# A 128-byte constant tile moved from ahead of the token tiles to behind them in on-chip memory

## The chip, the cores and the metric

The kernel runs on one core of one Trainium2 chip. The metric is the device time of one execution in microseconds; three runs of the kernel before were taken, and one more execution was profiled.

## The reference, cut to what matters

The reference takes 256 tokens of width 1024 (all fp32) through two transformer blocks.

```
def reference(x, ...):
    x = first_block(x, ...)    # norm; h @ w_in; mLSTM and sparse attention; two gated branches;
                               # @ w_out; norm; SwiGLU with a hidden width of 2816; final norm
    return second_block(x, mem, ...)  # norm; h @ w_in_2; linear attention, indexed attention,
                               # memory attention; three gated branches; @ w_out_2; norm;
                               # mixture of 16 experts
```

Nearly all arithmetic is products of 256 tokens with weight matrices that are read once from HBM. Each root-mean-square norm needs a power of minus one half, and that is the only use of the tile that the change moves.

## The kernel before, in words

**Slabs.** Each large weight matrix is streamed in slabs of 1024 rows by 256 columns, 1 MB each (`[P, KT, SW]`: 128 partitions by 8 pieces of the contraction by 256 columns, 8 KB in each partition). SyncE loads a slab into `ring`, ScalarE copies it rounded to fp32r into `w_hi` (`high`, line 578), VectorE writes the rest into `w_lo` (`low`, line 591), which lies on the memory of `ring`. The tokens are split in the same way into `xT_hi` and `xT_lo` (transposed: 128 partitions of features, 8 pieces, 256 tokens). A product is then three TensorE matmuls (`product`, line 616): hi by hi, hi by lo, lo by hi. All of them carry line 620 in the profile.

**Which operand stands and which moves.** In a matmul the stationary operand of 128 by 128 is loaded into the array by its own instruction (LDWEIGHTS, the row PEld), while the matmul ahead of it runs, and the moving operand of 256 or 512 columns streams past it. In the profile's names the moving one comes first: `bank<-xT_hi,w_hi` moves tokens past weights, `bank<-w_hi,xT_hi` moves weights past tokens. There are three ways to use a slab:

- `slab_rows` (line 627): weights stationary, tokens moving, 256 columns, 48 matmuls a slab. This is used for the query, key, merge, indexer and gate slabs, for gate and up of the first block's SwiGLU (`units_pe`, line 955), and with other moving tiles for the branch products: `ysT`, `o_m`, `o_g`, `o_d`.
- `slab_tokens` (line 642): tokens (or `mixT`, `merged`) stationary, weights moving, 256 columns, 48 matmuls.
- `slab_wide` (line 654): tokens or memory stationary, weights moving, 512 columns, 24 matmuls a slab.

The SwiGLU runs 11 units: a gate slab and an up slab by `slab_rows`, then a down slab whose moving weights pass the hidden tile `h` in 512 columns. The mixture of experts at the end does the same with gathered tokens `xgs`, `xgo` and `turned_h`, never with `xT`.

**Order.** It is written out by hand, in program order for each engine, with semaphores between them; there is no planner. TensorE's program starts at line 2546. SyncE issues the slab loads in the order of `STREAM`, each when the slab that held its slot has been used.

**Addresses.** Tiles that live all through the kernel are allocated one behind the other by `sb` (lines 153 to 177), and `place` (line 180) lays the other tiles over the memory behind `w_hi` at an offset. From the shapes, in bytes per partition: `ident` to `ones` take 4096 bytes, `minus_half` 128, `rows` and `cols` 1024 each, `x`, `xn`, `xT_hi` and `xT_lo` 8192 each, `ss` 64, then `w_lo` 32768 and `w_hi` 24576. So `xT_hi` begins at 22656 and `xT_lo` at 30848 (both 128 modulo 256), and `w_lo` at 39104 and `w_hi` at 71872 (both 192 modulo 256). All later tiles count from 96448, which is 192 modulo 256 too. Several of them carry hand-set offsets:

```
mixT_hi = place(64, "mixT_hi", [P, KT, T], F32R)
APART = [0, 0, 0, 64, 64, 64, 64, 64, 256, 256, 320]
EIGHT = [8 * KB + 8448 + 4608 + 8 * KB * i + APART[i] for i in range(11)]
```

With these, `o_m`, `o_g`, `o_d`, `merged`, `mixT_hi` and `ysT_lo` begin at 0 modulo 256, `mixT_lo` and `ysT_hi` at 128, and `h`, `memT`, `xgs`, `xgo` and `turned_h` at 192, as the weights do.

**The tile that moves.** `minus_half` is `[P, 32]`, 128 bytes. GpSimd fills it once (line 1160) and reads it in the roots of the norms (`norm_root`, line 746; `head_root`, line 938; line 1206). `x` and `xn` hold the tokens and their normed copy, which TensorE transposes into `xT`.

Of the kernel before, what the change touches and what calls it, by code (L numbers as in the profile page):

```python
# [14 lines left out]
P = 128  # L15
# [115 lines left out]
def program(nc, dram, out, plan):  # L131
# [3 lines left out]
    def sb(name, shape, dtype=F32, into=None):  # L135
        return (into or ctx).enter_context(nc.sbuf_tensor(name, shape, dtype))
# [23 lines left out]
    ones_r = sb("ones_r", [P, P], F32R)  # L160
    causal = sb("causal", [P, T])
    ones = sb("ones", [P, P])
    minus_half = sb("minus_half", [P, 32])
    rows = sb("rows", [P, 2, P])
    cols = sb("cols", [P, 2, P])
    x = sb("x", [P, TT, D])
# [3 lines left out]
        xT_raw = sb("xT_raw", [P, KT, T], into=into)  # L170
    xT_lo = sb("xT_lo", [P, KT, T], F32R)
    ss = sb("ss", [P, 8 * TT])
    raw_ctx = ExitStack()
    ring = sb("ring", [P, RAW, KT, SW], into=raw_ctx)
    raw_ctx.close()
# [2977 lines left out]
```

How the kernel before makes its waits and increments, by code:

```python
    def evicted(eng, s):  # L548
        for w in all_out(s):
            eng.wait_ge(*w)
# [1 line left out]
    def slab_out(eng, name, j=0):  # L552
        eng.wait_ge(slab_used, SLAB[name] + j + 1)
# [23 lines left out]
    def high(act, end):  # L578
        for s in range(split["hi"], end):
            act.wait_ge(*loaded(s))
            if HI <= s < MOE + HI:
                act.wait_ge(slab_used, s - HI + 1)
            elif MOE + HI <= s < MOE + MORE_HI:
                act.wait_ge(*moe_pe.done("gather", KT - 1))
            elif s >= HI:
                act.wait_ge(slab_used, s - MORE_HI + 1)
            for k in halves(s):
                act.activation(HIGHS[HI_SLOT[s]][:, k, :], RAWS[SLOT[s]][:, k, :], ACT.Copy).then_inc(w_hi_ready, 1)
        split["hi"] = max(split["hi"], end)
# [1 line left out]
    def low(vec, end):  # L591
        for s in range(split["lo"], end):
            for n, k in enumerate(halves(s)):
                vec.wait_ge(w_hi_ready, parts_of(s, n))
                vec.tensor_tensor(LOWS[SLOT[s]][:, k, :], RAWS[SLOT[s]][:, k, :], HIGHS[HI_SLOT[s]][:, k, :].bitcast(F32),
                                  ALU.subtract).then_inc(w_lo_ready, 1)
        split["lo"] = max(split["lo"], end)
# [8 lines left out]
    def slab_in(pe, s):  # L607
        pe.wait_ge(w_lo_ready, parts_of(s, 0))
        if s in BANKED and BANKED[s] >= 2:
            pe.wait_ge(bank_read[BANKED[s] % 2], 2 * (BANKED[s] // 2))
# [1 line left out]
    def second_half(pe, s):  # L613
        pe.wait_ge(w_lo_ready, parts_of(s, 1))
# [432 lines left out]
    @block.sync  # L1047
# [96 lines left out]
            if name == "kv":  # L1144
                sp.wait_ge(loads["rev"], 16)
```

## Time and profile before

| | us |
|---|---|
| median of 3 runs | 1015.41 |
| lowest and highest run | 1014.60 and 1018.62 |
| the profiled execution, its own time | 1016.27 |
| its span, first to last instruction | 1015.0 |
| TensorE matmuls busy in it | 995.4 (98%) |
| weight loads busy in it | 897.7 (88%) |
| VectorE, ScalarE busy in it | 680.8, 585.2 |
| mean granted TensorE clock | 0.997 of full speed |

The profile is one execution. Busy matmul time counts a matmul from its start to its modelled end, and matmuls overlap, so how fast TensorE goes is read from the distance between the starts of two matmuls (called the pace below), not from busy time or from the duration of one. 0.86 us lie between the profiled execution's own time and the median.

### The profile page before, as it was taken

The page shows a single profiled execution, that of the slowest core. Times are in us where ns is not written, and L with a number is a line of the kernel's source. Part 1 is how long each engine was busy: PE and PEld are TensorE (multiplying, and loading weights), DVE is VectorE, ACT ScalarE, POOL GpSimd, SP SyncE. Part 2 cuts the span into 40 slices and gives each one's busy share as a digit, 9 for nine tenths or more (in the row PEclk, how much of TensorE's full clock was granted, in tenths as well). Part 3 has the DMA queues.
Part 4 walks back from the last instruction along what each step waited for, and adds up shares of the span by engine and source line. Part 5 has one row for each costly group of instructions (what it writes and reads, how often), then busy time and mean ns, then how long its engine had stood idle before and what let it go on. Part 6 is the DMA issues. An engine that isn't in the chain of part 4 may idle for free.

```text
span 1015.0 us, 16341 instructions
## 1 busy us (share of the span) xinstructions
PE 995.4 (98%) x6730; PEld 897.7 (88%) x6730; DVE 680.8 (67%) x1019; ACT 585.2 (58%) x855; POOL 44.0 (4%) x57
## 2 busy tenths in 40 slices
PE   6999999999999999999999999999999989999998
PEld 6998988999999999889898878998999978888886
DVE  5865767677555545586575665656556768998887
ACT  5564576756343433374585545675444548877774
POOL 4101000000000000010010001100000000000001
PEclk9999999999999999999999999999999989999999
DMA  9994543357655556564453333553565928999995
GB/s 263 262 304 130 151 156 125 126 169 209 198 182 192 190 184 198 178 217 144 147 167 125 124 125 125 166 172 125 167 205 174 314 96 275 367 371 371 369 367 198
DMA packets 168248, 206.31 MB, mean 203 GB/s; under 512 B 11431, under 2 KB 143118, under 8 KB 168174
## 3 DMA queue, kind: packets, MB, share of 16 engines
q1 hardware_dynamic: 159598, 196.01, 59.3%
q0 software_dynamic: 2224, 6.07, 2.0%
q10 hardware_dynamic: 6352, 3.19, 1.2%
q8 instruction: 53, 0.87, 0.4%
q14 instruction: 21, 0.17, 0.1%
HBM read 201.56 MB, written 4.73 MB: 203 GB/s over the span
## 4 chain that ended last, share of the span: by engine, by line
PE 89%; DVE 3%; DMA 3%; ACT 2%; issue 1%; SPq 1%; POOL 0%; ACTq 0%; DVEq 0%; POOLq 0%
PE bank L620 76%; PE bank L757 1%; PE bank L813 1%; DVE w_lo L596 1%; DMA ring<-in_w_in 1%; PE bank L3038 1%; DMA ring<-in_w_up 1%; PE bank L803 1%; ACT w_hi L588 1%; PE bank L2631 1%; PE bank L2715 1%; DMA ring<-in_w_out 1%; PE bank L2770 1%; PE bank L2732 1%; DMA x<-in_x 1%
## 5 line engine op out<-in xcount | busy, mean ns | idle before, releaser
L596 DVE TENSOR_TENSOR w_lo<-ring,w_hi 128x1024 fp32r<-128x1024 f32 (+1 forms) x302 | 423.0, 1436 | 176.5 <-ACT w_hi L588 176.0
L588 ACT ACTIVATE w_hi<-ring 128x1024 fp32r<-128x1024 f32 (+1 forms) x302 | 357.6, 1225 | 184.4 <-PE bank L620 141.8
L620 PE MATMUL bank<-xT_hi,w_hi 128*128 128x256 f32 x896 | 253.4, 283 | 0.0
L620 PE MATMUL bank<-xT_lo,w_hi 128*128 128x256 f32 x896 | 250.8, 280 | 0.0
L620 PE MATMUL bank<-xT_hi,w_lo 128*128 128x256 f32 x896 | 250.8, 280 | 0.0
L620 PEld LDWEIGHTS bank<-xT_hi,w_hi 128*128 128x128 f32 x896 | 169.1, 189 | 2.5 <-issue 1.6
L620 PEld LDWEIGHTS bank<-xT_hi,w_lo 128*128 128x128 f32 x896 | 170.8, 191 | 0.0
L620 PEld LDWEIGHTS bank<-xT_lo,w_hi 128*128 128x128 f32 x896 | 169.0, 189 | 0.8 <-issue 0.2
L620 PE MATMUL bank<-w_hi,xT_hi 128*128 128x512 f32 (+1 forms) x208 | 77.7, 373 | 0.3 <-ACT cmp_in L1309 0.3
L620 PE MATMUL bank<-w_hi,xT_lo 128*128 128x512 f32 (+1 forms) x208 | 76.2, 366 | 0.0
L620 PE MATMUL bank<-w_lo,xT_hi 128*128 128x512 f32 (+1 forms) x208 | 75.8, 364 | 0.0
L620 PE MATMUL bank<-w_hi,xgs_hi 128*128 128x512 f32 x128 | 51.5, 402 | 0.0
L620 PE MATMUL bank<-w_hi,xgs_lo 128*128 128x512 f32 x128 | 50.1, 391 | 0.0
L620 PE MATMUL bank<-w_lo,xgs_hi 128*128 128x512 f32 x128 | 49.9, 390 | 0.0
L620 PEld LDWEIGHTS bank<-w_hi,xT_hi 128*128 128x128 f32 x208 | 39.1, 188 | 8.0 <-issue 1.9
L620 PEld LDWEIGHTS bank<-w_hi,xT_lo 128*128 128x128 f32 x208 | 39.1, 188 | 6.7
L620 PEld LDWEIGHTS bank<-w_lo,xT_hi 128*128 128x128 f32 x208 | 39.1, 188 | 6.2
L620 PE MATMUL bank<-w_hi,h_hi 128*128 128x512 f32 x88 | 34.2, 389 | 0.0
L620 PE MATMUL bank<-w_lo,h_hi 128*128 128x512 f32 x88 | 34.2, 389 | 0.0
L620 PE MATMUL bank<-w_hi,h_lo 128*128 128x512 f32 x88 | 34.2, 389 | 0.0
L620 PE MATMUL bank<-w_hi,turned_hi 128*128 128x512 f32 x80 | 31.2, 390 | 0.0
L620 PE MATMUL bank<-w_hi,turned_lo 128*128 128x512 f32 x80 | 31.1, 389 | 0.0
(549 smaller groups left out, 1797.3 us busy)
## 6 DMA issues: line engine op xcount, KB each, us to landing
ring<-in_w_in SPq DMA_DIRECT2D x54, 1024.0 KB, 5.2
ring<-in_w_down SPq DMA_DIRECT2D x31, 1024.0 KB, 7.1
ring<-in_w_gate SPq DMA_DIRECT2D x40, 512.0 KB, 7.3
ring<-in_w_up SPq DMA_DIRECT2D x40, 512.0 KB, 8.8
ring<-in_w_gate SPq DMA_DIRECT2D x11, 1024.0 KB, 5.3
ring<-in_w_up SPq DMA_DIRECT2D x11, 1024.0 KB, 5.4
ring<-in_w_out SPq DMA_DIRECT2D x8, 1024.0 KB, 5.1
ring<-in_w_mem_kv SPq DMA_DIRECT2D x8, 1024.0 KB, 5.1
```

The lines of the kernel that those rows point to most:

```text
L588: act.activation(HIGHS[HI_SLOT[s]][:, k, :], RAWS[SLOT[s]][:, k, :], ACT.Copy).then_inc(w_hi_ready, 1)
L596: vec.tensor_tensor(LOWS[SLOT[s]][:, k, :], RAWS[SLOT[s]][:, k, :], HIGHS[HI_SLOT[s]][:, k, :].bitcast(F32), ALU.subtract).then_inc(w_lo_r ...
L620: ins = pe.matmul(dst, a, b, start=(start and j + m == 0), stop=(stop and j == len(pairs) - 1 and m == 2), **kw)
L757: ins = pe.transpose(bank[4 + k // 2][:, at:at + P], src[:, t, k * P:(k + 1) * P], ident[:, :])
L803: ins = pe.matmul(dst, a, b, start=(i == 0), stop=(i == len(parts) - 1))
L813: ins = pe.matmul(dst, a, b, start=(i == 0), stop=(i == len(parts) - 1))
L2631: ins = mm_(bank[3][0:NG * NCMP, j * P:(j + 1) * P], blk[:, j, n, :, :].rearrange("p g c -> p (g c)"), w_cmp1[:, j, n, :], start=(n == 0), ...
L2715: ins = mm_(bank[4 + odd][:, i * K:(i + 1) * K], nqT[odd * ND:(odd + 1) * ND, h // 2, tt * P:(tt + 1) * P], kT[odd * ND:(odd + 1) * ND, br ...
L2732: ins = mm_(dst[odd], v_sw[:, kt, b, g * ND:(g + 1) * ND], aT[:, b, kt, 2 * odd:2 * odd + 2, :], start=False, stop=(b == 1 and kt == tt))
L2770: ins = pe.transpose(nsa_turned(u, kt)[:, i * P:(i + 1) * P], lg_nsa(u)[:, i, kt * P:(kt + 1) * P], ident[:, :])
L3038: ins = mm_(bank[GATHER_BANK[k]][:, :], v[:, t, k * P:(k + 1) * P], onehot[:, t, 0:NGRP, :].rearrange("p g s -> p (g s)"), start=(t == 0 a ...
```

## The change

`minus_half` is no longer allocated between `ones` and `rows`, but between `ss` and the weight ring. Nothing else differs: no instruction, wait, loop or shape.

```diff
@@ -160,7 +160,6 @@
     ones_r = sb("ones_r", [P, P], F32R)
     causal = sb("causal", [P, T])
     ones = sb("ones", [P, P])
-    minus_half = sb("minus_half", [P, 32])
     rows = sb("rows", [P, 2, P])
     cols = sb("cols", [P, 2, P])
     x = sb("x", [P, TT, D])
@@ -170,6 +169,7 @@
         xT_raw = sb("xT_raw", [P, KT, T], into=into)
     xT_lo = sb("xT_lo", [P, KT, T], F32R)
     ss = sb("ss", [P, 8 * TT])
+    minus_half = sb("minus_half", [P, 32])
     raw_ctx = ExitStack()
     ring = sb("ring", [P, RAW, KT, SW], into=raw_ctx)
     raw_ctx.close()
```

Seven tiles (`rows`, `cols`, `x`, `xn`, `xT_hi`, `xT_lo`, `ss`) begin 128 bytes lower, at 22528 and 30720 for the two token tiles (0 modulo 256). The weight tiles and everything behind them stay where they are.

## Rows read from the trace of the kernel before

**Rows 1.** The page: busy time by engine, then the chain that ended last.
```profile
PE 995.4 (98%) x6730; PEld 897.7 (88%) x6730; DVE 680.8 (67%) x1019; ACT 585.2 (58%) x855; POOL 44.0 (4%) x57
...
PE 89%; DVE 3%; DMA 3%; ACT 2%; issue 1%; SPq 1%; POOL 0%; ACTq 0%; DVEq 0%; POOLq 0%
```
**Rows 2.** The chain in order of time: start, us, what.
```profile
234.63 216.92 PE bank L620 x1464
...
712.73 94.05 PE bank L620 x816
```
**Rows 3.** Line 620 on TensorE, 239.9 to 428.9 (SwiGLU): ns min/median/max, first and last start.
```profile
L620 PE MATMUL bank<-xT_lo,w_hi x352: 281/281/281, 240.1 to 413.0; 128*128 128x256 f32 x176
```
**Rows 4.** TensorE's timeline, ends of four SwiGLU slabs (192 matmuls), then the down slab.
```profile
239.95 0.28 PE L620 MATMUL bank<-xT_hi,w_hi 128*128 128x256 f32 x1
...
262.44 0.28 PE L620 MATMUL bank<-xT_hi,w_lo 128*128 128x256 f32 x1
262.56 0.39 PE L620 MATMUL bank<-w_hi,h_hi 128*128 128x512 f32 x1
...
267.77 0.39 PE L620 MATMUL bank<-w_hi,h_lo 128*128 128x512 f32 x1
```
**Rows 5.** Line 620, 712.9 to 790.2 (gate and branch slabs by turns), columns as in rows 3.
```profile
L620 PE MATMUL bank<-xT_lo,w_hi x112: 276/276/279, 712.7 to 784.4; 128*128 128x256 f32 x112
...
L620 PE MATMUL bank<-o_d_lo,w_hi x64: 280/280/280, 751.4 to 790.0; 128*128 128x256 f32 x64
```
**Rows 6.** TensorE's timeline: ends of one branch slab and of one gate slab in there.
```profile
718.02 0.28 PE L620 MATMUL bank<-o_g_hi,w_hi 128*128 128x256 f32 x1
...
723.56 0.28 PE L620 MATMUL bank<-o_g_hi,w_lo 128*128 128x256 f32 x1
...
724.02 0.28 PE L620 MATMUL bank<-xT_hi,w_hi 128*128 128x256 f32 x1
...
729.01 0.28 PE L620 MATMUL bank<-xT_hi,w_lo 128*128 128x256 f32 x1
```
**Rows 7.** Line 620 in four other stretches: 55 to 66, 654 to 666, 673 to 678, 597 to 602.
```profile
L620 PE MATMUL bank<-xT_lo,w_hi x32: 276/276/281, 55.1 to 65.7; 128*128 128x256 f32 x32
...
L620 PE MATMUL bank<-xT_lo,w_hi x32: 281/281/281, 654.5 to 665.5; 128*128 128x256 f32 x32
...
L620 PE MATMUL bank<-o_m_lo,w_hi x16: 276/276/276, 673.1 to 678.2; 128*128 128x256 f32 x16
...
L620 PE MATMUL bank<-w_lo,xT_hi x16: 277/279/279, 596.7 to 602.0; 128*128 128x256 f32 x16
```
**Rows 8.** Groups by form: weights moving past tokens and past `merged`, mean ns last.
```profile
L620 PE MATMUL bank<-w_hi,xT_hi 128*128 128x512 f32 x160 | 64.0, 400 | 0.0
...
L620 PE MATMUL bank<-w_lo,merged_hi 128*128 128x256 f32 x64 | 17.7, 277 | 0.0
```
**Rows 9.** TensorE's timeline in a wide slab: weights moving past tokens, 42 matmuls apart.
```profile
535.03 0.39 PE L620 MATMUL bank<-w_lo,xT_hi 128*128 128x512 f32 x1
...
544.64 0.39 PE L620 MATMUL bank<-w_lo,xT_hi 128*128 128x512 f32 x1
```
**Rows 10.** Matmuls of tokens past weights in the whole trace, columns as in rows 3.
```profile
L620 PE MATMUL bank<-xT_lo,w_hi x896: 276/281/415, 12.9 to 784.4; 128*128 128x256 f32 x180
```
**Rows 11.** The view of the moved tile: its largest reader, columns as in rows 3.
```profile
L748 POOL TENSOR_TENSOR ss<-ss,minus_half x6: 695/705/1601, 7.7 to 818.5; 128x2 f32<-128x2 f32 x6
```
**Rows 12.** Windows: us, PE, PEld, DVE, ACT, POOL busy (count), clock, DMA share, GB/s.
```profile
234.60:451.50 216.90, 216.90 (x1467) 200.91 (x1465) 126.81 (x149) 97.01 (x123) 1.39 (x2) 1.00 0.61 194
712.70:806.80 94.10, 94.10 (x819) 94.10 (x818) 56.87 (x73) 43.60 (x57) 0.00 (x0) 1.00 0.66 212
850.00:971.00 121.00, 121.00 (x547) 99.17 (x545) 108.55 (x88) 94.53 (x86) 1.62 (x3) 1.00 1.07 368
```
**Rows 13.** TensorE's timeline at the start of a gate slab.
```profile
647.30 0.29 PE L620 MATMUL bank<-xT_lo,w_hi 128*128 128x256 f32 x1
...
647.55 0.28 PE L620 MATMUL bank<-xT_hi,w_hi 128*128 128x256 f32 x1
```

## The prediction

> **What bounds the kernel now.** I read the page first: TensorE's matmuls are busy for 98% of the span, and the chain of work that ended last is TensorE for 89% [rows 1]. The chain in order of time then shows stretches with nothing but line 620 in them, above all 216.92 us from 234.63 and 94.05 us from 712.73 [rows 2]. The windows over these say that no other engine is near its limit there: VectorE 127 of 217 us, DMA 0.61, and full clock [rows 12]. So whatever changes the pace of TensorE's matmuls there changes the end by as much. In the mixture of experts, DMA share is 1.07 [rows 12], but its matmuls read neither token tile except in a short gather, and its loads wait for slots that TensorE frees, so time won or lost ahead of it passes through.
>
> The change has no instruction in it, so the only thing to look for is whether the time of an operation depends on its addresses. The view of line 620 is to be read for that. One form of matmul, tokens past weights in 256 columns, has two durations in steady running, 276 and 281 ns, with a median of 281 over 896 [rows 10]. All 352 of the SwiGLU are at 281 exactly [rows 3], all of the gate slabs from 712.9 at 276 [rows 5]. The timeline turns this into paces. In the SwiGLU, from 239.95 to 262.44 there are 191 steps, 117.7 ns each [rows 4]. In the gate slab, 724.02 to 729.01 is 44 steps, 113.4 ns each [rows 6]. So the same form on the same tiles runs at a **fast pace** of 113.4 or a **slow pace** of 117.7 ns, 4.3 ns or 0.21 us for a slab of 48. Going by the starts of all slabs one by one, 20.2 of the 56 token slabs run fast: 8.2 of 16 ahead of the SwiGLU, none of its 22, 5 of the 11 between 458 and 712, all 7 from 712.9. A slab keeps its pace from a few matmuls after its start to its end: the two from 55 on are fast, the two from 654 on slow [rows 7]. Something set at the start of a run thus chooses between two paces, and a slab at 113.4 leaves nothing more to win.
>
> **What distance the tiles have.** I write r for moving minus stationary address modulo 256, in bytes. Tokens past weights have r = -64 now (128 against 192) and +64 after (0 against 192). Weights past tokens have +64 now and -64 after. Branch tiles past weights already have +64, weights past `merged` already have -64; both also agree with the tokens after the change modulo 1024. `h`, `memT` and the gathered tokens have 0 and keep it. So the trace of before already holds the two new distances, on other tiles, and the forecast can be made from those.
>
> **The change part by part.**
>
> *The tile itself.* GpSimd reads `minus_half` in thirteen small operations, six of them of about 0.7 us [rows 11]. They are the same after. I cost its new place at nothing either way; 128 bytes more or less in an address add no work to an operation of two columns. If even 0.1 us came on each, at most one microsecond would show, and part of that beside TensorE work.
>
> *Tokens past weights, slabs that are fast now.* Of slabs with r = +64, the branch slabs are one fast, `o_m` at 673 [rows 7], and eleven slow (`o_g`, `o_d` at 279 to 280 ns [rows 5], and from 718.02 to 723.56 47 steps of 117.9 ns [rows 6]). Of three slabs of weights past tokens in 256 columns, also +64, one is fast and two are slow, as the one from 597 to 602 [rows 7]. That makes 2 fast of 15. The bounds are that all 20.2 fast token slabs stay fast (0) and that all turn slow (20.2 x 0.21 = 4.2 us). I take the share of the branch slabs: 2.7 stay, 17.5 turn, **+3.7 us**.
>
> *Tokens past weights, slow now.* These are 35.8 slabs, 22 of them in the SwiGLU, where each pair follows the down slab with r = 0. No row shows a step from r = 0 to r = +64. Bounds: none turns fast (0), or all do (35.8 x 0.21 = -7.5 us; the SwiGLU alone -4.6). By the nearest rows, the 2 of 15, I take 4.7 slabs, **-1.0 us**.
>
> *Weights past tokens, 512 columns.* There are 480 such matmuls, three groups like the one of 160 [rows 8]. Their pace is 9.61 us over 42 steps, 228.8 ns [rows 9], against 5.21 over 23, 226.5 ns, with r = 0 [rows 4]. At most 2.3 ns each can go, 1.1 us. Nothing shows 512 columns at r = -64, so the other bound is that they get worse by as much. `merged` in 256 columns with r = -64 is at 277 ns on average [rows 8], fast for the three slabs that follow each other, so I lean to a gain and take half, **-0.5 us**.
>
> *Weights past tokens, 256 columns.* Three slabs, two slow now; at the rate of `merged` (three fast of four) this gives **-0.2 us**, between -0.4 and +0.2.
>
> *Everything else that moves.* `x` and `xn` are read in transposes and by VectorE and ScalarE, which have slack [rows 12]; I take 0. The waits stay the same, and ahead of each stall stands the same producer.
>
> Sum: +3.7 - 1.0 - 0.5 - 0.2 = **+2.0 us**. Against the profiled execution's own 1016.27 (span 1015.0, 1.3 around it) that is 1018.3. The median of the runs is 0.86 lower, so 1015.41 + 2.0 gives **1017.4**.
>
> **A page that speaks against any effect.** In this trace the same form has the paces 113.4 and 117.7 on the same tiles, and 228.8 against 226.5 on different ones [rows 4, 6, 9]. The Trainium skill, page "TensorE: Matmul & The Clock Gate", section "Step-by-step: what each phase is for", says that TensorE has two independent read ports, one for the moving operand and one for the weight load, so that the load takes no bandwidth from the running matmul. By that, the distance of two tiles could not matter and the sum would be 0. No row here shows the ports themselves; that the 512-column pace differs by tile in all fifteen runs of weights past tokens speaks against it.
>
> **The rivals.**
>
> *The fast pace wins in the SwiGLU.* The step from `h` or `memT` (r = 0) to tokens now always ends in the slow pace, 11 of 11, and the step from fast tokens (r = -64) to a branch tile (r = +64) too, 7 of 7. So what counts is phase and distance together, and a phase that clashes at -64 need not at +64. With tokens and branches at one distance, the back and forth from 718 on goes as well. If only the SwiGLU turns fast and the fast ones elsewhere turn slow: -4.6 + 3.7 - 1.1 - 0.2 (weights past tokens) = -2.2, 1013.2. If all 256-column slabs with tokens or branches run fast: -7.5 - 2.3 (eleven branch slabs) - 0.4 - 1.1 = -11.3, 1004.1. The middle is 1008.7. For it: 36 of 56 token slabs have something to win and only 20 to lose. Against it: 13 of 15 slabs with +64 are slow.
>
> *Nothing happens.* Distance has no say, and the pace is set by the waits alone, which stay: 1015.4. For it: the same tiles show both paces. Against it: the 7-by-7 alternation, which follows the tile at every boundary.
>
> *Slower, by a third pace.* The place is the SwiGLU. A gate slab shows 647.30 to 647.55 for two steps, 125 ns [rows 13], as it starts; it is gone after some matmuls, because it falls back. If r = +64 after r = 0 held that pace, the 22 slabs would lose 22 x 48 x 7.3 ns = 7.7 us: with the rest 1025. It decides the sign from 3 ns a matmul on (3.2 us, which brings the sum to 5.1). Against it: no slab holds this pace, at any distance.
>
> **How the numbers follow.** Forecast 0.43, fast SwiGLU 0.31, nothing 0.13, third pace 0.13. About 5 us, 0.5%, is what a measurement can tell from no change. The forecast's bounds are 1012 to 1020, nearly all of it within 0.5%. Of the 0.31, some 0.25 lies below 1010.3, since it needs more than the SwiGLU alone. Slower by over 0.5% are 0.12 of the third pace and 0.03 of the forecast. That makes faster 0.26, same 0.59, slower 0.15. The range from 1005 to 1021 leaves out the last of the all-fast case and most of the third pace, under 0.2 together; the forecast's own range is 1012 to 1020.
>
> **What would show each step.** In the profile after: the duration of tokens past weights over the SwiGLU (281 now; a value near 280 says slow at the new distance, 276 fast, above 285 the third pace), and its pace from the first and last start of a slab. From 712.9 on, whether gate slabs join the branch slabs at 279 to 280 or draw them to 276. The wide slabs: 226.5 or 228.8. The median of all 896. And the stretch of 216.92 us in the chain: 221 or more refutes the forecast on one side, under 214 on the other. Should all paces stay while the time moves, the cause is elsewhere, in the first load or in `xn`, and the whole working is wrong.

## The result, and the profile after

Ten runs of each kernel: before 1018.19 us in the median (1014.35 to 1019.23), after 1022.97 (1020.29 to 1023.99). The ratio is 1.006, with a 95% interval from 1.0048 to 1.0072: by it the change makes the kernel slower by 6.1 us (4.9 to 7.3). (The two medians lie 4.8 us apart and the two means 5.4, so 5 to 6 us is what these runs support.) The change was taken again at the end, as one of the experiments, and gave 1.0061. The prediction had no measurable change as likeliest, +2.0 us, with an upper end of its range at 1021. It was wrong: the measured 1022.97 lies 2 us above that end. (The median of before was 2.8 us higher in these ten runs than in the three that the prediction had. The two groups of times that the clock makes, below, are the likely reason, but no clock is on record for these ten; against those three, the ratio gives 1021.5, which is outside too.)

The instructions on each engine are the same and stand in the same order. The profiled execution has an own time of 1023.99 and a span of 1022.7, against 1015.0 before. The page of after, against [rows 1]: the engines' busy times and the chain by engine.

```profile
PE 1003.6 (98%) x6730; PEld 902.6 (88%) x6730; DVE 681.2 (67%) x1019; ACT 585.5 (57%) x855; POOL 44.2 (4%) x57
...
PE 94%; DMA 2%; DVE 2%; ACT 1%; issue 1%; SPq 1%; POOL 0%; DVEq 0%; ACTq 0%; POOLq 0%
```

VectorE, ScalarE and GpSimd are busy for the same time within 0.4 us, TensorE for 8.2 us more, with the same 6730 matmuls. So nearly all of the extra time lies in matmuls and not in waits.

The SwiGLU in the chain in order of time (start, us, what), against [rows 2]:

```profile
236.34 217.29 PE bank L620 x1464
```

It is 0.4 us longer only. The window over it (columns as in rows 12) says the same as [rows 12]: VectorE, ScalarE and DMA are far from their limits, at full clock.

```profile
236.00:455.00 219.00, 219.00 (x1483) 202.63 (x1481) 128.30 (x151) 98.67 (x125) 1.71 (x3) 1.00 0.61 193
```

Line 620 on TensorE: first the whole trace, then 241.5 to 431.6 (SwiGLU), then 716.7 to 795.9 (gate and branch slabs by turns). Columns as in rows 3; the answers to [rows 10], [rows 3] and [rows 5].

```profile
L620 PE MATMUL bank<-xT_lo,w_hi x896: 276/279/415, 12.9 to 790.1; 128*128 128x256 f32 x180
...
L620 PE MATMUL bank<-xT_lo,w_hi x352: 279/279/281, 241.7 to 415.1; 128*128 128x256 f32 x176
L620 PE MATMUL bank<-w_hi,h_hi x88: 389/389/402, 264.2 to 431.0; 128*128 128x512 f32 x88
...
L620 PE MATMUL bank<-xT_lo,w_hi x112: 278/280/280, 717.0 to 790.1; 128*128 128x256 f32 x112
L620 PE MATMUL bank<-o_d_lo,w_hi x64: 280/280/280, 756.5 to 795.7; 128*128 128x256 f32 x64
```

The SwiGLU stays slow (281 became 279, but that is the duration of one matmul, not the distance of starts: that comes below). The gate slabs from 717 on went from 276 to 280, all seven. Among the token slabs the fast pace is gone but for parts of two, at 160 and 167 us.

TensorE's timeline of after, as in [rows 4] and [rows 9]: the same matmuls by their number in the program, in the SwiGLU, at the start of the down slab behind it, and in a wide slab.

```profile
241.63 0.28 PE L620 MATMUL bank<-xT_hi,w_hi 128*128 128x256 f32 x1
...
264.13 0.28 PE L620 MATMUL bank<-xT_hi,w_lo 128*128 128x256 f32 x1
264.25 0.40 PE L620 MATMUL bank<-w_hi,h_hi 128*128 128x512 f32 x1
264.49 0.39 PE L620 MATMUL bank<-w_lo,h_hi 128*128 128x512 f32 x1
264.71 0.39 PE L620 MATMUL bank<-w_hi,h_lo 128*128 128x512 f32 x1
264.94 0.40 PE L620 MATMUL bank<-w_hi,h_hi 128*128 128x512 f32 x1
...
537.87 0.39 PE L620 MATMUL bank<-w_lo,xT_hi 128*128 128x512 f32 x1
...
547.67 0.39 PE L620 MATMUL bank<-w_lo,xT_hi 128*128 128x512 f32 x1
```

In the SwiGLU 22.50 us for 191 steps is 117.8 ns, exactly the slow pace of before. In the wide slab 9.80 us for 42 steps is 233.3 ns, where it was 228.8: **4.5 ns more on a matmul, and this was forecast to fall.** The down slab starts with steps of 240 and 220 ns, and its first eight are 231 ns in the mean, where its own pace is 227.

Summed over the trace, by the mean step of each form (steps inside slabs, stalls left out), after minus before: tokens past weights 116.3 to 117.7 ns, 2688 matmuls, +3.8 us; weights past tokens in 512 columns 229.3 to 233.3, 480 matmuls, +1.9; `h` 226.7 to 228.1, 264 matmuls, +0.4; one `o_m` slab +0.2; weights past tokens in 256 columns -0.2; `merged` -0.2. The sum is +5.9. The gate slabs' last matmul of tokens starts at 790.1 where it was 784.4 [rows 5], 5.7 us later. So the slabs account for the whole difference up to there.

The other 2 us of the span difference of 7.7 come after the last norm, and they go with the clock. Windows of after there (columns as in rows 12):

```profile
824.00:834.30 10.30, 6.64 (x19) 5.42 (x19) 7.86 (x21) 3.98 (x5) 1.10 (x1) 0.50 0.21 69
...
846.00:849.00 3.00, 3.00 (x19) 2.72 (x19) 2.09 (x7) 2.98 (x3) 0.39 (x1) 0.83 0.74 186
849.00:852.00 3.00, 3.00 (x9) 2.33 (x9) 1.75 (x1) 0.37 (x1) 1.12 (x2) 0.60 0.48 165
```

The same place of the profiled execution before:

```profile
820.80:827.60 6.80, 5.25 (x15) 4.33 (x16) 5.19 (x13) 1.22 (x4) 0.00 (x0) 0.50 0.01 2
...
828.00:866.00 38.00, 38.00 (x196) 31.95 (x195) 33.59 (x60) 29.80 (x35) 1.51 (x2) 1.00 0.64 217
```

TensorE waits around the norm and the router there (busy for 29.7 of 34 us from 800.0 in after, 28.7 of 33 from 795.0 in before), the granted clock falls to 0.50 (1.2 GHz), and it comes back to 1.00 (2.4 GHz) after 6.8 us in this execution of before and after 10.2 us, with a second dip of 3.4 us from about 848, in the one of after. The mean granted clock of a run, 0.997 for this execution of before and 0.993 for this one of after, varies from run to run in **both** kernels. Over all runs whose clock is on record, before has 35 runs at 0.997 with a mean of 1015.7 us, 33 at 0.993 with 1018.3, and 20 in between; after has 3 at 0.997 with 1020.6, 6 at 0.993 with 1023.7, and 8 in between. At equal clock the change costs 4.9 us in the one case and 5.3 in the other. Against the runs of before that were taken beside it, the repetition (e15 below) gives 5.5 us at 0.997 (2 runs against 9) and 5.8 at 0.993 (2 against 7). That is near the 5.9 of the slabs. Only 3 of the 17 runs of after had 0.997, and 35 of 88 of before; whether the change makes these rarer isn't shown by so few.

### The profile page after: what moved, and what is told of

The parts are those of the page before. It is cut to its first block, busy times and chain, and to the rows that moved or that the text cites. A ratio compares the mean times of both kernels' runs of the same rounds, so it can differ in the third digit from the quotient of the medians.

```text
span 1022.7 us, 16341 instructions
## 1 busy us (share of the span) xinstructions
PE 1003.6 (98%) x6730; PEld 902.6 (88%) x6730; DVE 681.2 (67%) x1019; ACT 585.5 (57%) x855; POOL 44.2 (4%) x57
## 4 chain that ended last, share of the span: by engine, by line
PE 94%; DMA 2%; DVE 2%; ACT 1%; issue 1%; SPq 1%; POOL 0%; DVEq 0%; ACTq 0%; POOLq 0%
PE bank L620 80%; PE bank L757 1%; PE bank L813 1%; PE bank L803 1%; PE bank L3038 1%; DMA ring<-in_w_up 1%; PE bank L2631 1%; PE bank L2715 1%; DMA ring<-in_w_out 1%; PE bank L2770 1%; PE bank L2732 1%; DMA x<-in_x 1%; SPq L1128 0%; PE bank L2940 0%; PE bank L2945 0%
## 5 line engine op out<-in xcount | busy, mean ns | idle before, releaser
L620 PEld LDWEIGHTS bank<-xT_hi,w_lo 128*128 128x128 f32 x896 | 168.7, 188 | 0.0
```

Source lines behind the costliest of these rows:

```text
L620: ins = pe.matmul(dst, a, b, start=(start and j + m == 0), stop=(stop and j == len(pairs) - 1 and m == 2), **kw)
```

## The experiments

In the theory after the result, the distance r of the moving from the stationary tile, modulo 256 bytes, sets which paces a matmul can have, and the tile's move costs through the tokens' r alone. Its rivals are the absolute place of the tiles; the place of `x`, `xn` or of `minus_half` itself; the entry into a slab rather than its distance. The experiments were run in four groups. Ratios are against runs of the kernel before in the same group; its median was 1017.47, 1016.37, 1017.17 and 1015.89 us in the four. Of each kernel one execution was profiled, and all paces come from that one. "The slabs' sum" is the sum by mean steps, as above. (The addresses given ahead of the prediction count from the first tile; only distances enter below.)

### First group: which tile, and is it distance?

**e1_all_up**: everything from `rows` on lies 128 bytes higher, all distances kept. The small tile `ik_sq`, which then found no room at its place, lies on other free memory in this and the other kernels that take up more.

```diff
+    sb("gap1", [P, 32])
-    ik_sq = place(EXTRA + 4 * KB, "ik_sq", [P, TT, IDIM])
+    ik_sq = place(EXTRA, "ik_sq", [P, TT, IDIM])
```

> Everything from rows on lies 128 bytes higher than before, so the tokens have the absolute address class they have after the change, but their distance to the weights is that of before (-64). Theory 1 (the distance of tokens to weights modulo 256 sets the pace): same as before, ratio 0.998 to 1.002, about 20 of 56 token slabs fast, wide slabs at 228.9 ns. Theory 2 (the address of the tokens itself counts): ratio 1.006, all token slabs slow, wide slabs at 233.3 ns. (ik_sq, one small tile, lies on the memory of score to make room.)

Measured: 0.9975 (0.9965 to 0.9985), not slower. Its tokens keep their two paces, against [rows 10] and, below, [rows 8]:

```profile
L621 PE MATMUL bank<-xT_lo,w_hi x896: 276/281/287, 12.7 to 783.1; 128*128 128x256 f32 x180
...
L621 PE MATMUL bank<-w_hi,xT_hi 128*128 128x512 f32 x160 | 64.1, 401 | 0.0
```

20.1 of 56 token slabs are fast (20.2 before), and the wide slabs take 229.6 ns (229.3). The absolute place modulo 256 isn't the cause. The 2.4 us that it gained in the median are not in the slabs (their sum is -0.2 us) and partly in the clock: at 0.997 the difference is 1.4 us (1014.9 against 1016.3). What the rest is stays open (e14 below has the same shift).

**e2_x_xn**: `minus_half` between `xn` and `xT_hi`, so `rows`, `cols`, `x` and `xn` move, and the token tiles don't.

```diff
-    minus_half = sb("minus_half", [P, 32])
     rows = sb("rows", [P, 2, P])
...
     xn = sb("xn", [P, TT, D])
+    minus_half = sb("minus_half", [P, 32])
```

> minus_half stands between xn and xT_hi: only rows, cols, x and xn lie 128 bytes lower, the token tiles and weights stay. Theory 1: ratio 0.998 to 1.002, token slabs as before. Theory 3 (the new place of x and xn, whose transposes precede many stretches, sets the pace that follows): ratio 1.004 or more, and the slabs that follow transposes slow.

Measured: 1.0011 (0.9995 to 1.0028). The wide slabs take 229.2 ns; 13.5 instead of 20.2 token slabs are fast, +0.9 us by the slabs' sum. Neither the tile's own place nor that of `x` and `xn` makes the change's cost. But the choice between the two paces is touched by something other than distance: the seven gate slabs from 711 us on, fast in every other profile with the tokens at -64, are all slow in this one. One profiled execution can't tell whether the place of `x` and `xn` does that or the execution.

**e3_hi_only**: `minus_half` between `xT_hi` and `xT_lo`: only `xT_hi` goes to r = +64.

```diff
+    minus_half = sb("minus_half", [P, 32])
     xT_lo = sb("xT_lo", [P, KT, T], F32R)
```

> minus_half stands between xT_hi and xT_lo: x, xn and xT_hi lie 128 lower, xT_lo stays, so two of three matmuls have the new distance and one the old. Theory 1: if each matmul pays for its own distance, two thirds of the loss, ratio 1.004, wide slabs at about 231.8 ns (two thirds of the way from 228.9 to 233.3). If the mixture itself decides, as in ysT (hi -64, lo +64 for moving tiles), all moving token slabs at 117.8 and a ratio near 1.005.

Measured: 1.0045 (1.0031 to 1.0059), 4.6 us, with 4.9 by the slabs' sum. No token slab is at 113.4 ns: 24 run at 117.0, among them all 22 of the SwiGLU, and 32 at 117.8. The wide slabs take 231.7 ns. Two thirds of the matmuls read `xT_hi`, and three quarters of the change's cost by the ratios (4.6 of 6.1 us) are there.

**e4_r0**: the tokens at the distance zero from the weights.

```diff
+    sb("gap1", [P, 16])
...
     ss = sb("ss", [P, 8 * TT])
+    sb("gap2", [P, 48])
```

> Tokens and weights at one place modulo 256 (r = 0), as h and memT are. Theory 1 by the rows of before: wide slabs fall from 228.9 to 226.7 ns (-1.1 us); the token slabs of 256 columns are open: all fast would be -7.5 us more (ratio 0.992), all slow +4.2 (ratio 1.003). Theory 2: at least as slow as after or unrelated.

Measured: 1.0067 (1.0041 to 1.0093). The timeline of this kernel, the same matmuls as in [rows 4] and [rows 9]:

```profile
242.78 0.28 PE L622 MATMUL bank<-xT_hi,w_hi 128*128 128x256 f32 x1
...
265.69 0.28 PE L622 MATMUL bank<-xT_hi,w_lo 128*128 128x256 f32 x1
...
541.22 0.39 PE L622 MATMUL bank<-w_lo,xT_hi 128*128 128x512 f32 x1
...
550.76 0.39 PE L622 MATMUL bank<-w_lo,xT_hi 128*128 128x512 f32 x1
```

119.9 ns in 256 columns, worse than either pace of before; 227.1 ns in 512 columns, better than before. This is the clearest result for distance: one shift moves the two forms in opposite directions, and the wide slabs take the pace that `h` has at r = 0 (226.7).

### Second group: modulo what, and are other tiles alike?

**e5_r128**: r = 128 for the tokens. **e6_plus_256**: the weights and all behind them 256 bytes up.

```diff
-    minus_half = sb("minus_half", [P, 32])     # e5
+    minus_half = sb("minus_half", [P, 16])
...
+    sb("gap2", [P, 16])
...
     ss = sb("ss", [P, 8 * TT])                 # e6
+    sb("gap2", [P, 64])
```

> minus_half 64 bytes long and 64 bytes behind ss: tokens 128 from the weights (r = 128 = -128), everything behind ss in place. Theory 1 (distance modulo 256, a table of paces by r: tokens moving 116.3 ns on average at -64, 117.8 at +64, 119.9 at 0; weights moving in 512 columns 226.7 at 0, 228.9 at +64, 233.3 at -64): a fourth entry, different from the others on both. If only the fraction of 64 mattered (theory 4), it would equal r = 0: 119.9 and 227.

> Weights and all behind them 256 bytes higher, tokens in place: distance -64 - 256. Theory 1 with 256 as the modulus: as before, about 20 token slabs fast, wide slabs 228.9 ns, ratio 0.998 to 1.002. If the modulus is 512 or more, other paces, wide slabs away from 228.9.

Measured: e5 1.0083 (1.0055 to 1.0112), 119.3 ns and 232.6 ns. e6 0.9995 (0.9977 to 1.0013), 116.3 ns and 229.3 ns, the paces of before to the tenth of a nanosecond. So 256 bytes are a period of the effect (64 is not one, by e4, nor 128, by the change itself).

**e7_h_plus64**: the tokens as before, the hidden tile `h` moved from 0 to +64.

```diff
-    h_hi, h_lo = (place((4 + 2 * i) * KB, "h_" + n, [P, 2, T], F32R) for i, n in enumerate(("hi", "lo")))
+    h_hi, h_lo = (place(EXTRA + 128 + 2 * KB * i, "h_" + n, [P, 2, T], F32R) for i, n in enumerate(("hi", "lo")))
```

> Before, with only the SwiGLU's hidden parts h_hi and h_lo in another place, where weights past h have r = +64 instead of 0. Theory 1 with the entry: what runs ahead decides which pace the tokens take. Before, the wide slabs with r = +64 were followed by token slabs twice, and both went fast; slabs with r = 0 were followed by slow ones 11 of 11 times. So the 22 SwiGLU slabs turn fast (-4.6 us) and h pays 264 x 2.3 ns (+0.6): ratio 0.996. If the entry doesn't matter, the SwiGLU stays at 117.8 and the ratio is 1.001.

Measured: 1.0004 (0.999 to 1.0019). Line 620 on TensorE, 262 to 429:

```profile
L620 PE MATMUL bank<-xT_lo,w_hi x289: 280/281/282, 261.7 to 413.1; 128*128 128x256 f32 x145
...
L620 PE MATMUL bank<-w_hi,h_hi x87: 392/392/398, 262.0 to 428.4; 128*128 128x512 f32 x87
```

`h` takes nearly the steady pace of the tokens at that distance, 229.1 ns against 228.8 (229.8 in the mean, 226.7 before). So 512 columns at +64 cost 2.2 to 2.5 ns more than at 0 on both tiles. And the SwiGLU's tokens, which now follow slabs at +64, are still all slow: the tile ahead does not decide it. The query-key slab at 66 us turned slow and the token slab at 108 fast, though `h` is first read at 262: which of the two paces a slab takes can differ without any change of its distance.

**e8_branch_minus64**: the branch tiles moved to the tokens' old distance, r = -64.

```diff
-    APART = [0, 0, 0, 64, 64, 64, 64, 64, 256, 256, 320]
+    APART = [0, 0, 0, 192, 192, 192, 192, 192, 256, 256, 448]
-    merged_lo = place(EIGHT[4], "merged_lo", [P, KT, T], F32R)
+    merged_lo = place(EIGHT[4] - 128, "merged_lo", [P, KT, T], F32R)
-    merged_hi = place(EIGHT[6], "merged_hi", [P, KT, T], F32R)
+    merged_hi = place(EIGHT[6] - 128, "merged_hi", [P, KT, T], F32R)
```

(`w_hi_more` and `xgs` take 192 off where they took 64, so that they stay.)

> Before, with the branch results o_m, o_g, o_d 128 bytes further, so that as moving tiles they have r = -64, the distance that tokens have; merged and the gathered tokens keep theirs. Theory 1: the distance works on any tile, so the eight branch slabs from 705 on turn fast as the gate slabs between them, -1.7 us, ratio 0.998, duration 276 instead of 279 to 280. Rival: the pace belongs to something else in the branch slabs, and they stay at 117.8.

Measured: 1.0000 (0.9984 to 1.0016). All eight slabs of `o_g` and `o_d` went fast, from 117.8 to 113.4 ns (-1.7 us); the one fast `o_m` slab turned slow, and `merged`, whose distance is unchanged, fell from three fast slabs of four to an average of 117.3 (+0.5). So a branch tile can hold the fast pace at -64, but part of the win was lost by the choice between two paces elsewhere. That the distance of the branch tile itself made them fast isn't shown: in e11 of the next group seven of the same eight slabs are fast too, with their distance left at +64.

### Third group: the table by distance

**e9_r_m32, e10_r_m96, e11_r_p32, e12_r_p96**: the tokens at -32, -96, +32 and +96, by paddings ahead of `rows` (gap1) and behind `ss` (gap2), which leave the weights where they were or 256 bytes up, for example e11:

```diff
+    sb("gap1", [P, 24])
...
     ss = sb("ss", [P, 8 * TT])
+    sb("gap2", [P, 40])
```

(e9 has 8 and 56; e10 shortens `minus_half` to `[P, 24]` with 8 behind; e12 puts 8 in the place of `minus_half` and `[P, 16]` of it with 8 more behind `ss`.)

> Tokens 32 bytes below the weights (r = -32 for moving tokens). Theory 1a (between the measured distances the pace lies between theirs): moving tokens on average between 116.3 (-64) and 119.9 (0), about 118.1 ns; wide slabs, r = +32, between 226.7 and 228.9, about 227.8; time about +3 us against before, ratio 1.003. Theory 1b (only whole steps of 64 bytes matter, the lower or the upper neighbour): either the numbers of -64 or those of 0 on both.

> Tokens 96 bytes below the weights (r = -96). Theory 1a: moving tokens between 116.3 (-64) and 119.3 (128), about 117.8 ns; wide slabs between 228.9 and 232.6, about 230.7; ratio 1.004. Theory 1b: the numbers of -64 or those of 128.

> Tokens 32 bytes above the weights (r = +32). Theory 1a: moving tokens between 119.9 (0) and 117.8 (+64), about 118.8 ns; wide slabs, r = -32, between 226.7 and 233.3, about 230; ratio 1.005. Theory 1b: the numbers of 0 or those of +64.

> Tokens 96 bytes above the weights (r = +96). Theory 1a: moving tokens between 117.8 (+64) and 119.3 (128), about 118.5 ns; wide slabs between 233.3 and 232.6, about 233; ratio 1.007. Theory 1b: the numbers of +64 or those of 128.

Measured, with the other runs in one table. "By paces" is the sum over all forms as in the first section, "by ratio" the ratio of the runs times 1015.4, and "equal clock" the difference of mean times against before in the same group, at the mean clock that has the most runs of the kernel (in brackets: runs of the kernel, runs of before; the row of after uses e15 there). r is that of tokens past weights; weights past tokens have minus r. "Steady" are the paces to which the 56 token slabs settle.

```
kernel   r     tokens past w   steady        w past tokens   by paces   by ratio (95%)         equal clock
               256 col, ns     ns            512 col, ns     us         us                     us
before  -64    116.3           113.4, 117.8  229.3
e4        0    119.9           120.0         227.6           + 9.8      + 6.8 ( 4.2 to  9.4)   + 8.3 (3, 9)
e11     +32    116.9           116.7, 117.8  233.2           + 3.2      + 1.0 (-0.3 to  2.2)   + 2.1 (6, 5)
after   +64    117.7           117.8         233.3           + 6.0      + 6.1 ( 4.9 to  7.3)   + 5.5 (2, 9)
e12     +96    120.0           120.0         234.2           +12.6      +11.9 (10.1 to 13.8)   +11.8 (3, 6)
e5      128    119.3           118.7, 119.9  232.6           +10.3      + 8.4 ( 5.6 to 11.4)   + 9.5 (4, 12)
e10     -96    118.3           117.3, 118.7  233.3           + 9.0      + 7.7 ( 5.4 to 10.2)   + 8.7 (2, 6)
e9      -32    118.3           118.3         233.3           + 7.8      + 7.9 ( 5.6 to 10.2)   + 7.9 (3, 6)
```

The fast pace of 113.4 ns is held by about 20 token slabs before and by no whole token slab at any other distance; after has it in parts of two. The sum by paces lies above the ratio's interval for e4 and e11, and within 1.5 us of the difference at equal clock for all.

Line 622 of e11 on TensorE, 715 to 792 (columns as in rows 3), against [rows 5]: the slabs of `o_g` and `o_d`, whose distance is +64 as before, are fast from 721 on, all seven.

```profile
L622 PE MATMUL bank<-o_d_lo,w_hi x63: 276/276/276, 753.9 to 791.8; 128*128 128x256 f32 x63
...
L622 PE MATMUL bank<-o_g_lo,w_hi x48: 276/276/276, 720.7 to 747.9; 128*128 128x256 f32 x48
```

They give e11 1.4 us of its sum back. So +64 allows the fast pace as -64 does, and what a slab takes there depends on more than its own distance; here the gate slabs between them run at 116.7.

The timelines of e11 and of e12, the same stretch of the SwiGLU as in [rows 4]; first e11, 22.29 us for 191 steps, 116.7 ns:

```profile
241.35 0.28 PE L622 MATMUL bank<-xT_hi,w_hi 128*128 128x256 f32 x1
...
263.64 0.28 PE L622 MATMUL bank<-xT_hi,w_lo 128*128 128x256 f32 x1
```

Then e12, in the SwiGLU and in the wide slab of [rows 9]; 120.0 ns, and 9.84 us for 42 steps, 234.3 ns:

```profile
243.36 0.28 PE L622 MATMUL bank<-xT_hi,w_hi 128*128 128x256 f32 x1
...
266.29 0.28 PE L622 MATMUL bank<-xT_hi,w_lo 128*128 128x256 f32 x1
...
542.71 0.39 PE L622 MATMUL bank<-w_lo,xT_hi 128*128 128x512 f32 x1
...
552.55 0.39 PE L622 MATMUL bank<-w_lo,xT_hi 128*128 128x512 f32 x1
```

Both theories of the expectations fail: the paces neither run evenly between their neighbours nor go in steps of 64 bytes: 32 bytes from -64, in either direction, is slow. For 512 columns there are two good distances, 0 and +64 of weights from tokens, and every other one tried costs 232.6 to 234.2. For 256 columns the old distance, -64, has the best mean of the eight, because there token slabs fall into the fast pace of 113.4; +32 has a third stable pace of 116.7 all through the SwiGLU. Of the eight distances tried, the kernel before lies at the one that is good for both forms.

### Fourth group: a version better than both

**e13_branch_merged**: as e8, without the two lines of `merged`, so that weights move past it at +64. **e14_branch_merged_up**: the same with e1's 128 bytes ahead of `rows`. **e15_after_again**: the change once more.

```diff
-    APART = [0, 0, 0, 64, 64, 64, 64, 64, 256, 256, 320]
+    APART = [0, 0, 0, 192, 192, 192, 192, 192, 256, 256, 448]
```

> Before with the branch results at the tokens' distance (-64, as in the run before this kind) and merged at +64 for the weights that move past it. Theory: the eight branch slabs from 705 on stay fast (-1.7 us); merged follows fast slabs, and if +64 suits it as the query-key slabs of weights past tokens at 66, its three slabs in a row are fast again (-0.6): ratio 0.998. Rival: merged goes slow at +64 as most slabs do there, and the ratio stays near 1.000.

> The same with everything from rows on 128 bytes higher, the shift that by itself gave a ratio of 0.9975. If that shift gives something of its own, the two add to 0.996; if its gain was the share of executions with the shorter half-speed stretch of TensorE's clock, the ratio equals that of the kernel without the shift, and the extra shows only in the mean clocks of its runs.

> The changed kernel once more beside before on one chip. Theory 1: in runs of equal mean clock (0.997, or 0.993) it is 5 us slower, which the paces of its slabs give; the rest of the 6 us is the share of runs with the lower clock. Rival: the loss itself is a clock loss, and at equal clock the two kernels are within 2 us.

Measured: e13 0.9987 (0.9972 to 1.0001), 1014.72 against 1015.89 us. e14 0.9991 (0.9976 to 1.0006), so the gain of e1's shift does not come back in the ratio; eight of its 12 runs had the lower clock of 0.993, and against before at that clock it is 2.3 us faster (8 runs against 7). e15 1.0061 (1.0039 to 1.0082), with the paces 117.6, 233.3 and 228.1 ns, where the first profile of after has 117.7, 233.3 and 228.1. One token slab, at 116 us, is at 113.4 here and was at 117.8 there: in the same kernel the choice between the two paces can differ from one execution to the next. Line 620 of e13 from 711 to 790, against [rows 5]:

```profile
L620 PE MATMUL bank<-xT_lo,w_hi x112: 276/276/282, 711.2 to 781.6; 128*128 128x256 f32 x112
...
L620 PE MATMUL bank<-o_d_lo,w_hi x64: 276/276/276, 749.3 to 787.1; 128*128 128x256 f32 x64
```

With branch and gate slabs at one distance, both run at 276: from the first start of tokens to the last of `o_d` it is 75.9 us, where it was 77.3 (712.7 to 790.0). At a clock of 0.997 e13 takes 1013.6 (6 runs) against 1015.3 (9 runs) for the kernel before in the same group; eight slabs by 0.21 us are 1.7. The interval of the ratio still touches 1, so that e13 beats the kernel before is likely and not shown; the change it beats by 0.7%, by the two ratios of this group.

## Why the prediction was wrong

*What bounds the kernel* was right: TensorE's pace alone moved, and each slower matmul came out at the end.

*The tile itself*, 0: right. Its reads in the roots take 696/705/1603 ns, where they took 695/705/1601 [rows 11], and e2 has no measurable cost.

*Fast token slabs turning slow*, +3.7 us: right. About 19 of 20.2 turned, and the tokens' mean step gives +3.8. But the forecast had 2.7 slabs stay fast, by the share 2 in 15, and no whole one did.

*Slow token slabs turning fast*, -1.0: didn't happen; no whole slab turned. The share of 2 in 15 was a poor guide. This second failed term is 1 us of the miss.

*The wide slabs*, -0.5 us between bounds of 1.1 either way: **this is the step that failed**. They cost +1.9 us, outside the bound, which is 2.4 us of the miss of about 4. The prediction said that "nothing shows 512 columns at r = -64, so the other bound is that they get worse by as much". That bound had no row behind it: it mirrored a possible gain. The two paces that the trace of before does hold, 226.5 at r = 0 and 228.8 at +64, are the two best of the eight distances, so any new one could only be worse, by 3.3 to 4.9 ns (e5, e12). And the hint from `merged`, 256 columns at -64 and fast, didn't carry over to 512 columns, as e4 shows from the other side: r = 0 is nearly the worst for one width (119.9 ns) and the best for the other (227.6).

*Weights past tokens in 256 columns*, -0.2: right, two of three slabs are fast now, where one was. The one at 600 (after) is at 276, where it was 277 to 279 [rows 7].

*Everything else*, 0: it missed `h`. Its distance did not change, and its steady pace did not either, but a down slab that follows tokens at the new distance starts unevenly (240 and 220 ns above, and 231 in the mean of eight steps), which costs 1.4 ns a matmul in the mean, 0.4 us in all. Ten of the eleven down slabs do this; the last follows a slab of `memT`, which has r = 0 too, and does not. `x` and `xn` at 0 hold within what e2 can tell.

The sum by these steps is +3.8 for tokens past weights, +1.9 for the wide slabs, +0.4 for `h`, +0.2 for one `o_m` slab, and -0.2 each for weights past tokens in 256 columns and for `merged`: +5.9 where the forecast had +2.0.

*The rivals.* The SwiGLU didn't turn fast (117.8 ns as before), and e7 shows that the slab ahead isn't what keeps it slow. "Nothing happens" fell by e1 and e6, which keep the distances and the paces, against after, e3 and e4. The third pace isn't in the SwiGLU at +64; slower came by another way. It does exist, at other distances: 116.7 at +32, 119.9 to 120.0 at 0 and +96.

*The page.* The Trainium skill's independent read ports ("TensorE: Matmul & The Clock Gate", section "Step-by-step: what each phase is for") would have given no effect. The runs disagree: the same matmuls take 229.3, 227.6 or 234.2 ns in 512 columns as the distance of their two operands changes (before, e4, e12). The measurement decides. No run shows the ports, nor which of the two operands' reads is the one delayed, so why the distance matters stays open.

*The chances.* Slower by over 0.5% had 0.15, because 0.12 of it was hung on one mechanism in the SwiGLU, and the unknown cost of the widest form was given a bound of 1.1 us. With a bound from the largest spread of paces seen between any two states (4.4 ns for 256 columns, or twice that in 512), the 480 wide matmuls could have cost 2.1 to 4.2 us, and the forecast's own range would have reached 1021 to 1023.

## What to carry to other kernels

Where matmuls follow each other without a gap, as in this kernel, the placement of the two operands is a parameter worth a sweep: here it moved the whole kernel by 1.2% (e12) with not one instruction changed, and 256 bytes of padding alone cost nothing that was measured (e6, 0.9995). Sweep each form by itself (width, and which operand moves), since what is best for one was nearly the worst for another (e4), and look at the distances of starts of matmuls, not at their durations. If the trace of before holds only some of the states that a change can reach, and the kernel was settled on them, the states that it doesn't hold are to be given a wider bound on the bad side than on the good.

## What the runs showed of the hardware

- The step of back-to-back fp32r matmuls in this kernel depends on the distance of moving and stationary operand modulo 256 bytes in a partition: in 256 columns steady paces of 113.4, 116.7, 117.3, 117.8, 118.3, 118.7 and 119.9 to 120.0 ns; in 512 columns means of 226.7 (`h`) to 227.6 (tokens) at 0, a steady 228.8 to 229.1 at +64, and means of 232.6 to 234.2 at the rest.
- At one distance a run of matmuls can hold either of two paces, 113.4 and 117.8 ns at -64 and at +64, 117.3 and 118.7 at -96, 118.7 and 119.9 at 128, and nearly always keeps it to its end. What chooses is open: not only the distance, not the tile ahead alone (e7); e2, e8 and e11 shifted it without touching the distance of the slabs concerned, and in after and e15, one kernel, one slab differs.
- The slow clock after the router's wait lasts 6.8 us in the profile of before, 10.2 and then 3.4 us in that of after, and 6.8 and then 3.4 us in that of e15, the same kernel as after. The times of the kernel before at the mean clocks 0.997 and 0.993 lie 2.6 us apart, which is half of what is to be measured here. Runs compared at equal mean granted clock gave 4.9 to 5.8 us for the change.
